# Seventeen of 22 gate/up pairs by seven half-width products that add up in PSUM, all low parts made on VectorE, and the first two down tiles row by row

## What is computed

```python
def swiglu_ffn(h, w_gu, w_down):            # h (512, 1024), w_gu (1024, 2*2816), w_down (2816, 1024)
    gate, up = jnp.split(h @ w_gu, 2, axis=-1)
    return (jax.nn.silu(gate) * up) @ w_down
x = x + 0.5 * swiglu_ffn(rms_norm(x, norm_g[i, 0]), ffn_w_gu[i, 0], ffn_w_down[i, 0])   # FFN 0 and FFN 2
x = x + 0.5 * swiglu_ffn(rms_norm(x, norm_g[i, 2]), ffn_w_gu[i, 1], ffn_w_down[i, 1])   # FFN 1 and FFN 3
```

## Time and profile before

| | |
|---|---|
| three runs | 2178.32, 2178.50, 2178.51 us; median 2178.5 |
| span of the profiled execution, first to last instruction | 2176.6 us |
| the profiled execution's own device time | not recorded beside its span; the median of the runs is 1.9 us more than the span |
| granted TensorE clock, mean | 1.000 of full speed |
| chain of waits, by engine | PE 90%, DVE 5%, ACT 3%, DMA 1% |

### The profile page before, as it was taken

One profiled execution on the slowest core, in us unless ns is written; L12 is line 12 of the kernel. 1 busy time (PEld: TensorE's weight loads), 2 busy tenths in 40 slices (PEclk: granted clock), 3 DMA queues, 4 the chain that ended last, 5 costly groups with the idle time before them and its releaser, 6 DMA issues.

```text
span 2176.6 us, 31752 instructions
## 1 busy us (share of the span) xinstructions
PE 2159.6 (99%) x12728; PEld 1814.8 (83%) x12728; DVE 1589.7 (73%) x2449; ACT 1093.2 (50%) x1716; POOL 284.1 (13%) x244
## 2 busy tenths in 40 slices
PE   9999999999999999999999999999999999999999
PEld 7889897777778898988899997777788898977777
DVE  6779586988657696865787777777667795965873
ACT  5535254667545252435344346777545252538672
POOL 3101013000131011131010122000131010130000
PEclk9999999999999999999999999999999999999999
DMA  7556454131136666443755452222135565532211
GB/s 213 145 136 158 118 136 136 40 98 59 59 93 168 172 156 159 109 139 83 193 117 149 115 143 95 75 76 95 50 87 159 125 161 126 134 109 78 78 59 39
DMA packets 250235, 252.58 MB, mean 116 GB/s; under 512 B 5776, under 2 KB 236304, under 8 KB 250088
## 3 DMA queue, kind: packets, MB, share of 16 engines
q1 hardware_dynamic: 207184, 206.06, 29.6%
q0 software_dynamic: 41664, 40.05, 12.1%
q10 hardware_dynamic: 1240, 4.43, 0.5%
HBM read 213.79 MB, written 6.32 MB: 101 GB/s over the span
## 4 chain that ended last, share of the span: by engine, by line
PE 90%; DVE 5%; ACT 3%; DMA 1%; issue 1%; POOL 0%; SPq 0%; DVEq 0%; ACTq 0%
PE ps L1950 89%; DVE sb_wlo L1315 1%; PE ps L1954 1%; ACT sb_whi L765 1%; DMA sb_raw<-w_ada 0%; DVE sb_gla_ek L1656 0%; DMA sb_ffn_al<-sb_ffn_u 0%; DVE sb_gla_eq L1659 0%; ACT sb_xh L765 0%; DMA sb_xT<-xT 0%; DVE sb_xT L1444 0%; ACT sb_hyb_th L765 0%; DVE sb_gla_xb L1651 0%; DVE sb_gla_cf L1648 0%; DVE sb_gla_d L1636 0%
## 5 line engine op out<-in xcount | busy, mean ns | idle before, releaser
L1950 PE MATMUL ps<-sb_xh,sb_whi 128*128 128x512 f32 (+1 forms) x1888 | 679.1, 360 | 1.8 <-DVE sb_xl L1739 0.8
L1950 PE MATMUL ps<-sb_xl,sb_whi 128*128 128x512 f32 (+1 forms) x1888 | 662.6, 352 | 0.6 <-DVE sb_xl L1335 0.6
L1950 PE MATMUL ps<-sb_xh,sb_wlo 128*128 128x512 f32 (+1 forms) x1888 | 660.4, 352 | 0.0
L765 ACT ACTIVATE sb_whi<-sb_raw 128x1024 fp32r<-128x1024 f32 (+1 forms) x368 | 378.8, 1034 | 379.8 <-PE ps L1950 366.1
L1950 PEld LDWEIGHTS ps<-sb_xh,sb_whi 128*128 128x128 f32 x1888 | 357.2, 189 | 66.7 <-issue 18.5
L1315 DVE TENSOR_TENSOR sb_wlo<-sb_raw,sb_whi 128x1024 fp32r<-128x1024 f32 (+1 forms) x256 | 332.7, 1303 | 100.1 <-ACT sb_whi L765 98.6
L1950 PEld LDWEIGHTS ps<-sb_xl,sb_whi 128*128 128x128 f32 x1888 | 357.5, 189 | 50.8 <-DVE sb_xl L1335 3.5
L1950 PEld LDWEIGHTS ps<-sb_xh,sb_wlo 128*128 128x128 f32 x1888 | 357.2, 189 | 49.1
L1950 PE MATMUL ps<-sb_ffn_ah,sb_whi 128*128 128x512 f32 x704 | 275.4, 391 | 0.8 <-DMA sb_ffn_al<-sb_ffn_u 0.8
L1950 PE MATMUL ps<-sb_ffn_ah,sb_wlo 128*128 128x512 f32 x704 | 274.1, 389 | 0.0
L1950 PE MATMUL ps<-sb_ffn_al,sb_whi 128*128 128x512 f32 x704 | 273.9, 389 | 0.0
(11 more groups left out here) (293 smaller groups left out, 2838.2 us busy)
## 6 DMA issues: line engine op xcount, KB each, us to landing
sb_raw<-ffn_w_gu SPq DMA_DIRECT2D x86, 1024.0 KB, 5.2
sb_raw<-ffn_w_down SPq DMA_DIRECT2D x32, 1024.0 KB, 5.9
sb_ffn_al<-sb_ffn_u POOLq DMA_DIRECT2D x76, 256.0 KB, 4.0
sb_raw<-sb_raw POOLq DMA_DIRECT2D x56, 256.0 KB, 4.2
sb_raw<-w_ada SPq DMA_DIRECT2D x12, 1024.0 KB, 9.2
sb_raw<-ffn_w_down SPq DMA_DIRECT2D x16, 768.0 KB, 4.9
sb_raw<-gla_w_in SPq DMA_DIRECT2D x12, 1024.0 KB, 5.4
sb_raw<-diff_w_in SPq DMA_DIRECT2D x12, 1024.0 KB, 5.2
```

Source lines behind the costliest of these rows:

```text
L765: return e.activation(out, in_, func, bias=bias, scale=scale)
L1950: return e.matmul(out, lhsT, rhs, start=start, stop=stop, skip_group_check=skip)
```

## The change

- FAST becomes j = 5 to 21, so pairs 7, 15 and 21 of each FFN are fast too: 68 fast pairs in place of 56.
- The seven products take three banks. Product six adds onto one (in `run`), seven onto that, three onto five (`five_three`). Before each of these ScalarE copies what the bank half holds (`t_cap`), since others need it by itself. VectorE then needs two additions, `join_gate` (after the sixth product, three, four being under way) and `join_up` (at the start of the next pair), in place of four.
- All low parts are made by `low_part` on VectorE; the negated copies and the 76 adding DMAs go. GpSimd's queue issues only `gates_onto_ups`.
- The first two down tiles of each part are computed side by side, row t of tile 0, then row t of tile 1.
- FFN 3 no longer leaves two banks of the ring out. Counted from 0, an FFN used to put its last down tile (last part, m = 7) at place 81 of the ring, bank 7, in FFN 3 two further; now all four put it at place 84, bank 4. The first pair of FFN 2 takes places 0 and 1, banks 4 and 5.

```diff
-FAST = ((5, 6, 8, 9, 10, 11, 12, 13, 14, 16, 17, 18, 19, 20),) * 4
+FAST = (tuple(range(5, 22)),) * 4
...
             for part, (k0, n) in enumerate(FF_PARTS[f]):
-                p += 2 * (f == 3 and part == 1)
                 jobs = [("pair", j, 3 if j in FAST[f] else 2) for j in range(k0, k0 + n)]
...
 # ScalarE, a pair
                         if j in FAST[f]:
                             i = fast_before[f] + FAST[f].index(j)
-                            used(w, u)
+                            run, two_three, four = (psum[b] for b in f_banks[f]["pair", j])
+                            w.wait_ge(sem["t_prod"], 3 * i + 1)
                             if i >= 2:
-                                w.wait_ge(sem["f_join"], 4 * i - 7)
-                            act(first_product(sums, i), psum[FFN_NORM][...], ACT.Copy).then_inc(sem["t_act"], 1)
-                            if j > k0 and j - 1 in FAST[f]:
-                                silu(j - 1)
+                                w.wait_ge(sem["f_join"], 2 * i - 3)
+                            act(one_v[i % 2][:, 0, :], run[:, 0:256], ACT.Copy).then_inc(sem["t_cap"], 1)
+                            if j > k0:
+                                split(j - 1)
                             w_hi(u + 1)
+                            w.wait_ge(sem["t_prod"], 3 * i + 2)
+                            if i:
+                                w.wait_ge(sem["f_join"], 2 * i)
+                            act(four_five[:, 1, :], two_three[:, 256:512], ACT.Copy).then_inc(sem["t_cap"], 1)
+                            used(w, u + 1)
+                            act(one_v[i % 2][:, 1, :], run[:, 0:256], ACT.Copy).then_inc(sem["t_cap"], 1)
                             w_hi(u + 2)
-                            if j > k0 and tail_late(j - 1):
-                                split(j - 1)
                             w_hi(u + 3)
+                            w.wait_ge(sem["t_prod"], 3 * i + 3)
+                            act(four_five[:, 0, :], four[:, 0:256], ACT.Copy).then_inc(sem["t_cap"], 1)
+                            silu(j)
                             u += 4
                             continue
...
+                    w_hi(u)
+                    split(k0 + n - 1)
...
 # VectorE, a pair
-                        if after_fast:
-                            join_rest(f, j - 1, u - 4, vgw[(j - 1) % 2], ub[(j - 1) % 2][:, :], up_free)
-                            scale_gate(f, j - 1, vgw[(j - 1) % 2])
+                        if j > k0 and j - 1 in FAST[f]:
+                            join_up(f, j - 1, u - 4, joined, ub[(j - 1) % 2][:, :], up_free)
+                            product(j - 1, None)
...
                         w_lo(u)
+                        w_lo(u + 1)
+                        if j > k0:
+                            low_part(j - 1)
+                        if j in FAST[f]:
+                            join_gate(f, j, u, joined, gb[j % 2])
+                            scale_gate(f, j, gb[j % 2])
                             w_lo(u + 2)
-                            join_first(f, j, u, vgw[j % 2])
                             w_lo(u + 3)
...
-                    low_part(k0 + n - 1)
+                    j = k0 + n - 1
+                    join_up(f, j, u - 4, joined, ub[j % 2][:, :], up_free)
+                    product(j, None)
+                    w_lo(u)
+                    low_part(j)
...
+            def join_gate(f, j, u, joined, g):
+                i = fast_before[f] + FAST[f].index(j)
+                two_three = psum[f_banks[f]["pair", j][1]]
+                used(w, u + 2)
+                w.wait_ge(sem["t_cap"], 4 * i + 3)
+                e.tensor_tensor(g, joined[0][i % 2].rearrange("p k c -> p (k c)"), two_three[:, :],
                                 ALU.add).then_inc(sem["f_join"], 1)
+            def join_up(f, j, u, joined, up, up_free):
+                i = fast_before[f] + FAST[f].index(j)
                 used(w, u + 3)
+                w.wait_ge(sem["t_cap"], 4 * i + 4)
+                up_free(j)
+                run = psum[f_banks[f]["pair", j][0]][:, 0:256]
+                e.tensor_tensor(halves(up), run.unsqueeze(1).broadcast_to([128, 2, 256]), joined[1][:, :, :],
                                 ALU.add).then_inc(sem["f_join"], 1)
...
 # TensorE, down tiles
                     for m in range(KT):
                         b = f_banks[f]["down", (part, m)][0]
-                        bank_free(b)
-                        for k in range(0, n, 8):
-                            rows(u, 0, W.units[u][2], b, AH, AL, ("f_al", 22 * f + k0), k == 0, k + 8 >= n, k)
-                            u += 1
+                        H, L, ready = AH, AL, ("f_al", 22 * f + k0)
+                        if m == 0:
+                            pair = [f_banks[f]["down", (part, k)][0] for k in range(2)]
+                            for q in pair:
+                                bank_free(q)
+                            for t in range(n):
+                                for k in range(2):
+                                    rows(u + k, t, t + 1, pair[k], H, L, ready, t == 0, t == n - 1)
+                        elif m > 1:
+                            bank_free(b)
+                            rows(u, 0, n, b, H, L, ready, True, True)
+                        u += 1
...
 # TensorE, a fast pair
                 lo_done(w, u)
-                product(one, slots[0], 0, of_x(0, early), 0)
-                product(two, slots[0], 4, of_x(4, early), 4).then_inc(sem["w_used"], 1)
+                product(run, slots[0], 0, of_x(0, early), 0, True, False).then_inc(sem["t_prod"], 1)
+                product(two, slots[0], 4, of_x(4, early), 4, True, True).then_inc(sem["w_used"], 1)
                 lo_done(w, u + 1)
-                product(five, slots[1], 0, of_sums(0), None)
-                product(six, slots[1], 4, of_sums(2), None).then_inc(sem["w_used"], 1)
+                product(five_three, slots[1], 0, of_sums(0), None, True, False).then_inc(sem["t_prod"], 1)
+                w.wait_ge(sem["t_cap"], 4 * i + 1)
+                product(run, slots[1], 4, of_sums(2), None, False, False).then_inc(sem["w_used"], 1)
                 lo_done(w, u + 2)
-                product(three, slots[2], 0, of_x(4, late), 4).then_inc(sem["w_used"], 1)
+                w.wait_ge(sem["t_cap"], 4 * i + 2)
+                product(five_three, slots[2], 0, of_x(4, late), 4, False, True).then_inc(sem["w_used"], 1)
                 lo_done(w, u + 3)
-                product(seven, slots[3], 0, of_sums(1), None)
-                product(four, slots[3], 4, of_sums(3), None).then_inc(sem["w_used"], 1)
+                product(four, slots[3], 4, of_sums(3), None, True, True).then_inc(sem["t_prod"], 1)
+                w.wait_ge(sem["t_cap"], 4 * i + 3)
+                product(run, slots[3], 0, of_sums(1), None, False, True).then_inc(sem["w_used"], 1)
```

More of the change, by code:

```diff
@@ L669, in build, with halves @@
         t_before = [4 * sum(bool(FAST[k]) for k in range(f)) for f in range(5)]
-        t_act_before = [3 * t_before[f] + fast_before[f] for f in range(5)]
+        t_act_before = [3 * t_before[f] for f in range(5)]
         def tail_late(j):
             return j >= 4 and j not in (7, 15, 21)
-        def first_product(sums, i):
-            return sums[:, 12 + 2 * (i % 2):14 + 2 * (i % 2), :].rearrange("p a b -> p (a b)")
+        def halves(ap):
+            return ap.rearrange("p (k c) -> p k c", k=2)
         def ffn_banks(f):
@@ L698, in build @@
                 for j in range(k0, k0 + n):
[L699 to L709 removed]
+                    n_vec += 1
+                    low_done[22 * f + j] = "f_al", n_vec
         def h_evac(w, k):
@@ L1465, in x_sums @@
                 w.wait_ge(sem["t_vec"], 4 * n + 2)
-                e.tensor_tensor(out[:, 3, :], out[:, 2, :], y[:, 2, :], ALU.add).then_inc(sem["t_vec"], 1)
-            def halves(f, j):
-                return fast_before[f] + FAST[f].index(j), [psum[b][:, :].rearrange("p (k c) -> p k c", k=2)
-                                                           for b in f_banks[f]["pair", j]]
-            def join_first(f, j, u, vgw):
-                i, (six_two, _, _) = halves(f, j)
-                one = first_product(ffn_mem[f][5], i)
-                used(w, u + 1)
-                w.wait_ge(sem["t_act"], 3 * t_before[f + 1] + i + 1)
-                e.tensor_tensor(vgw[:, 0:2, :], one.unsqueeze(1).broadcast_to([128, 2, 256]), six_two,
+                e.scalar_tensor_tensor(out=out[:, 3, :], in0=out[:, 2, :], scalar=-1.0, in1=y[:, 2, :], op0=ALU.mult,
+                                       op1=ALU.subtract).then_inc(sem["t_vec"], 1)
@@ L2067, in fast_pair, with product @@
                 i = fast_before[f] + FAST[f].index(j)
-                one = psum[FFN_NORM][:, 256 * (i % 2):256 * (i % 2) + 256]
-                (six, two), (three, seven), (four, five) = ([psum[b][:, 0:256], psum[b][:, 256:512]] for b in banks)
```

(10 more changed lines are left out.)

129 lines of the change are left out of this document (38 added, 91 removed).

## The result

| | before | after |
|---|---|---|
| median | 2178.41 us (4 runs, 2178.32 to 2178.51) | 2193.38 us (4 runs, 2192.53 to 2194.73) |
| span of the profiled execution | 2176.6 us | 2192.9 us (device time 2194.73) |
| granted TensorE clock, mean | 1.000 | 0.997 |

The ratio is 1.0070, 95% interval 1.0055 to 1.0084: slower by 0.7%, 15 us. That lies outside the range of 2169.5 to 2184.5; "slower" had been given a chance of 0.19.

What follows compares the result with a forecast made beforehand. TensorE's instructions were taken to bound the kernel inside the FFNs. The terms -10.0 - 0.9 + 8.3 + 1.8 gave -0.8 us, span 2175.8, and with 1.9 us from span to median 2177.7; range 2169.5 to 2184.5.

Steps and rivals of the forecast that it cites:

- What is saved: Twelve plain pairs become fast, 10.0 us, and the wait for an adding DMA goes, 0.9 us; together 10.9 us.
- Fast pairs, ScalarE: In fast pairs, ScalarE's copies come before the products that need them, product three being the tight one; cost 0.
- Rival 2: Copies come too late in fast pairs, before product three; 0.2 us a pair gives 2191; slower, chance 0.14.
- Fast pairs, VectorE: VectorE has 0.3 to 0.4 us less per fast pair; plain pairs swap a ScalarE copy for `low_part`; cost 0.
- The ends of FFNs: First down tile added 2.26 us later, carried to the ends of FFNs 0 to 2: 1.0, 5.1, 2.2; sum 8.3 us.
- Rival 1: FFN ends don't come late, as the ring has slack; 2170.3 or 2168.5; faster, chance 0.24 with partial forms.
- The w_ada panel: FFN 1, part 0: slots free later, loads beside the 4 MB copy; cost 1.8 us, bounds 0 and 4.

Runs made afterwards that it cites:

- e11: e10 with the old 14 fast pairs an FFN, FFN 3's two banks left out again and FFN 2's ring where it was; 2181.21 us.
- e10: Changed kernel with the edits of e6 and e12, and the 4 MB copy at the end of FFN 2 as in e9; 2170.10 us.
- e5: Changed kernel with VectorE's low parts of plain pairs moved into its gap and unit fb's low part before pair 4's product; 2190.32 us.
- e4: Changed kernel with ScalarE's two early copies in pair 5 put ahead of the SiLU and split of pair 4; 2193.76 us.
- e12: Changed kernel with e1's ring and the first two down tiles one after the other, except one row in the last part; 2182.02 us.
- e2: Changed kernel with the last part's first two down tiles computed one after the other; parts 0 and 1 stay side by side; 2187.96 us.
- e9: Changed kernel with the 4 MB copy moved from pair 7 of FFN 1 to the end of FFN 2; 2187.68 us.
- e8b: Changed kernel with the old list of 14 fast pairs an FFN and the two banks that FFN 3 left out; 2192.09 us.
- e3b: Changed kernel with FFN 1's 4 MB copy issued two pairs later, at j == 9; 2196.72 us.
- e1: Changed kernel with FFN 2's ring of banks starting one place further; 2189.63 us.
- e6: Changed kernel with the edits of e4 and e5 together; 2188.74 us.

## Why the prediction was wrong, by its own steps

**What is saved: right.** 10.08 us for a fast pair in every undisturbed stretch, no wait for `sb_ffn_al`; e11 against e10 shows the 10 us whole.

**Fast pairs, ScalarE: the step that failed.** "Cost 0. It stays 0 as long as ScalarE is less than 1 us late" was worked out for a fast pair that follows a fast pair, and is right there. The pair that follows a plain one has another queue before its first copy: the SiLU of the plain pair is done at its place in the next one, and waits for VectorE. That cost 7.8 of the 17.1 us by which the span missed the forecast (2192.9 against 2175.8). The deadline that broke was not product three, which I had called the tight one, but product six, whose copy I had given 2.9 us from ready to wanted. The trace of before had the answer, the copy 5.2 us after pair 5's start and behind that SiLU; I had read pair 10 only the earlier trace rows. Rival 2 named this mechanism and its sign, but before product three and as a price on all 68 pairs (and its 68 x 0.07 is 4.8 us, not 4.5).

**Fast pairs, VectorE: right for fast pairs, wrong for "Plain pairs get a `low_part` ... 0".** The low part and the ScalarE copy that went are not in the same queue. Moving it into VectorE's gap in e5, with one low part of a weight earlier, gives back 0.7 us an FFN, in sum 2.7 of the 7.8. As e4 alone gives nothing and the two together 5.7, the cost can't be shared out between the two engines.

**The ends of FFNs: the mechanism right, the size short of the clock.** 7.71, 29.32 and 37.76 us against 7.68, 29.33 and 37.8. Without the clock the three ends cost 8.9 us, forecast 8.3. Half clock behind the stalls added 3.7, a term that the sum didn't have. e12 shows that all of it hung on the first tile's late end and on one place of the ring. Rival 1 (the ring has slack) is refuted by e2: 2.26 us earlier at the start were 2.4 less at the wait. Its lateness of 2.1 us in each of FFNs 0 to 2 was misread for FFN 0, where VectorE's last addition came 1.2 us after TensorE had left the down tiles. The Trainium skill, "SBUF — State Buffer", section "Who interferes with whom", says that a VectorE instruction with two SBUF inputs and a GpSimd instruction that reads SBUF contend for a shared port. No run here tests whether that is what makes these steps slow; the forecast needed only the measured steps.

**The w_ada panel: the first half right, the second mis-sized.** The panel landed at 723.5 (716 to 722 was forecast, for down tiles that began at 702.3 and not at 704.9), and the waits behind it were 1.2 us. "Delays pair 8's sums by about 4 us against 11 of margin" was wrong in both numbers. SP's queue stands still until a slot is free, and the low parts that free it stand behind the panel on VectorE, so all of the panel's delay went on to four gate/up loads and the adding DMA: against TensorE, which was 1.8 us later than before at the down tiles, the sums came 13.4 - 1.8 = 11.6 us later. The margin was that of the low part of unit fa, done at 740.4 and wanted at 748.2 in the kernel before: 7.8. That costs 3.1 us and a fall of the clock. e9 shows the copy as the cause of both (loads of 5.2 and 7.7 us). In e8b, with pair 7 plain, the panel's load stood beside the copy too (19.5 us) but landed 8.5 us after the down tiles' start and not 18.6, and nothing waited for it. During the copy its queue and SP's moved 203 and 201 packets in 715 to 720, so the turn-taking was as forecast.

**Left open.** 0.4 us of the 16.3 were not followed up. Of the 0.6 us too much at the end of FFN 0, some 0.5 lie in the four matmuls behind the wait: 0.99 us from 365.44 to 366.43, where all 32 took 3.58 before. e11 stands 2.7 us above the kernel before. In its profile pairs 5 to 7 of the four FFNs take 2.4 us more than before and the last down tiles 0.6 more, and the wait for the adding DMA, 1.0 with its restart, is gone; no run tests why. e8b has a wait of its own, 0.9 us in FFN 3, which was not followed up either.

## What to carry to other kernels

A new wait must be priced at the first and the last iteration of a loop and at each change of kind, not in its steady state: find in the old trace when the thing that it will wait for is ready at those places. When something that was read at leisure becomes a deadline, its old lateness is the price. And when a stretch is cut to what its loads and its side engines can just bear, look for the one large transfer that can be put elsewhere before cutting: here it decided between +0.1% and -0.4%.

## What the runs showed of the hardware

**Stalls can be paid twice.** TensorE's granted clock, whole in all of the kernel before but for its very end, went to 0.5 behind or in three stalls of the changed kernel (3.1, 4.9 and 1.9 us of waiting) and gave 5.2 us of extra time, a third of the slowdown. A stall's length alone doesn't tell whether it happens. The wait of 1.8 us in FFN 2's pair 5 was followed by no fall in the changed kernel, e3b and e12, and by one in e1, e2 and e9. The wait of about 3 us before FFN 1's pair 8 was followed by one in the changed kernel, e1, e2 and e5, and by none in e6 (2.9 us). In e12 the clock fell even behind two waits of 0.8 and 0.5 us in FFN 1's first down tiles, where two of 0.8 and 0.5 in e2 had no such effect. e8b, with two waits of 1.9 at FFN ends and four of 0.7 to 1.6 in pairs 5, kept a mean clock of 1.000 in its profile. The runs of each kernel whose clock fell in its profile spread over 1.4 to 3.7 us. Those of e10 and e11, where it didn't, spread over 0.2 and 0.4; e8b's over 2.0, with a mean clock of 0.999 in the longest of them.

**Half of the DMA engines.** With the 4 MB copy among the fast pairs in e3b, the DMA engines' busy share stands at 5 tenths for a long stretch (40 slices of 765 to 800 us), though loads and adding DMAs were waited for (each digit is the mean busy share of the core's DMA engines in a slice, in tenths):

```profile
DMA  9999999555555554555557999999999994000099
```

The Trainium skill, "DMA: Bandwidth & Descriptors", section "Why a DMA increments its semaphore by 16 and not by 1", gives 8 engines for a leading dimension of 8. This row agrees: where e10 makes its loads without a copy beside them, from 697 to 704, the share stands at 9 tenths.
